# A two-block transformer kernel on one Trainium2 core: the latent attention's input projection taken in two passes over its token tiles, its weights split in the stage in front

## The reference

```python
x = first_block(...)                      # its last step: rms_norm(x_lat, final_g)
for l in range(2):                        # second block
    h = rms_norm_2(x, attn_norm[l])
    proj = h @ w_in[l]                    # gates | latent attention | rwkv | convolution
    c_q, c_kv, k_pe = split(mla_cols, [384, 256, 32])     # 672 columns
    o_a = mla_branch(...)                 # causal attention from c_q, c_kv, k_pe
    ...                                   # o_b: rwkv, o_c: short convolution, gated merge, w_out
    h2 = rms_norm_2(x, mlp_norm[l])
    x = x + square(relu(h2 @ w_up[l])) @ w_down[l]
```

## Time and profile before

| | |
|---|---|
| median of three executions | 4408.32 us |
| the profiled execution: its own time / its span | 4410.29 / 4408.5 us |
| TensorE busy (matmuls / weight loads) | 3905.1 us (89%) / 3036.3 us (69%) |
| VectorE, ScalarE, GpSimd busy | 1842.1 (42%), 1316.5 (30%), 430.7 us (10%) |
| mean granted TensorE clock | 0.926 of full |
| the chain that ended last | PE 74%, DVE 13%, ACT 6%, DMA 3%, POOL 2% |

### The profile page before, as it was taken

One profiled execution on the slowest core, in us unless ns is written; L12 is line 12 of the kernel. 1 busy time (PEld: TensorE's weight loads), 2 busy tenths in 40 slices (PEclk: granted clock), 3 DMA queues, 4 the chain that ended last, 5 costly groups with the idle time before them and its releaser, 6 DMA issues.

```text
span 4408.5 us, 52575 instructions
## 1 busy us (share of the span) xinstructions
PE 3905.1 (89%) x21392; PEld 3036.3 (69%) x21392; DVE 1842.1 (42%) x2826; ACT 1316.5 (30%) x1960; POOL 430.7 (10%) x277
## 2 busy tenths in 40 slices
PE   7788888999997898999788879899988887989999
PEld 3555547888886777788566657678866664767887
DVE  2544433533343334444533254543333335454433
ACT  3332323322233323322324321232232432123222
POOL 0211211000002110000111211000011121100000
PEclk8878889999998999999899989899999998999999
DMA  4112252121121222222111211123311120113332
GB/s 156 55 52 77 77 201 77 48 72 63 58 61 54 78 87 78 86 96 96 54 54 35 74 29 39 49 93 96 96 64 52 36 76 24 44 36 96 93 98 67
DMA packets 320320, 317.03 MB, mean 72 GB/s; under 512 B 8720, under 2 KB 286128, under 8 KB 319952
## 3 DMA queue, kind: packets, MB, share of 16 engines
q1 hardware_dynamic: 320080, 313.67, 22.5%
HBM read 311.55 MB, written 2.10 MB: 71 GB/s over the span
## 4 chain that ended last, share of the span: by engine, by line
PE 74%; DVE 13%; ACT 6%; DMA 3%; POOL 2%; issue 2%; SPq 0%; DVEq 0%; ACTq 0%; POOLq 0%
PE PS L132 73%; DVE scr L146 5%; ACT scr L142 4%; DMA ring<-in_ada_w 1%; DVE PS L160 1%; DVE NBt L156 1%; DVE scr L156 1%; DMA scr<-in_na_bias 1%; PE PS L135 1%; POOL na_w L146 1%; DVE scr L168 1%; DVE scr L164 1%; ACT L142 0%; DVE scr L152 0%; DVE scr L176 0%
## 5 line engine op out<-in xcount | busy, mean ns | idle before, releaser
L132 PE MATMUL PS<-scr 128*32 128x32 f32 (+7 forms) x6692 | 660.2, 284 | 133.7 <-DVE scr L146 77.8
L132 PEld LDWEIGHTS PS<-scr 128*128 128x128 f32 (+4 forms) x6692 | 538.1, 170 | 280.3 <-issue 126.0
L132 PE MATMUL PS<-ffn_h,ffn_w 128*128 128x512 f32 (+1 forms) x3168 | 615.5, 357 | 8.5 <-DVE ffn_h L156 5.7
L132 PEld LDWEIGHTS PS<-ffn_h,ffn_w 128*128 128x128 f32 x3168 | 524.2, 189 | 101.0 <-issue 9.7
L142 ACT ACTIVATE scr<-PS 128x256 f32<-128x256 f32 (+4 forms) x489 | 231.4, 473 | 1015.9 <-PE PS L132 946.7
L146 DVE TENSOR_TENSOR scr<-scr 128x512 f32<-128x512 f32 (+3 forms) x419 | 284.3, 678 | 282.5 <-ACT scr L142 246.6
L132 PE MATMUL PS<-h_h,ring_r 128*128 128x512 f32 (+1 forms) x976 | 365.4, 435 | 40.6 <-POOL ring_r L146 26.0
L132 PE MATMUL PS<-mlp_h,mlp_w 128*128 128x512 f32 x1536 | 364.3, 399 | 5.5 <-DVE mlp_h L146 5.0
L132 PE MATMUL PS<-mlp_g,mlp_w 128*128 128x512 f32 x1536 | 359.7, 396 | 0.0
L132 PEld LDWEIGHTS PS<-mlp_h,mlp_w 128*128 128x128 f32 x1536 | 291.3, 190 | 79.9 <-issue 9.4
L132 PEld LDWEIGHTS PS<-mlp_g,mlp_w 128*128 128x128 f32 x1536 | 288.5, 188 | 69.9
(11 more groups left out here) (150 smaller groups left out, 4739.4 us busy)
## 6 DMA issues: line engine op xcount, KB each, us to landing
ring<-in_ada_w SPq DMA_DIRECT2D x48, 1024.0 KB, 6.8
ring<-in_ffn_w_in SPq DMA_DIRECT2D x44, 1024.0 KB, 5.0
ring<-in_w_up SPq DMA_DIRECT2D x32, 1024.0 KB, 5.5
ring<-in_w_down SPq DMA_DIRECT2D x32, 1024.0 KB, 5.1
ring<-in_w_in SPq DMA_DIRECT2D x60, 512.0 KB, 3.9
ring<-in_ffn_w_out SPq DMA_DIRECT2D x16, 1024.0 KB, 5.0
scr<-in_na_bias SPq DMA_DIRECT2D x32, 512.0 KB, 5.6
ring<-in_na_w_qkv SPq DMA_DIRECT2D x24, 512.0 KB, 4.1
```

The costliest lines, as they stand in the source:

```text
L132: return self.eng.matmul(o, lhsT=l, rhs=r, start=start, stop=stop) if self.eng else Nothing()
```

## The change

`mla_pe` takes the token tiles in two passes: j = 0 and j = 1 for tiles 0, 1, 2, then j = 0 and j = 1 for tile 3 (whose banks it takes and waits for only there), then j = 2 for all four, in the order 3, 0, 1, 2. `mi_k` j now fires when tile 3 has used j. DVE and ACT take the tiles out in the same order 3, 0, 1, 2. `final_pe` puts its sums in banks 4 and 5 and its rows in 6 and 7. The copies (ACT) and subtractions (POOL) of j = 0 and 1 move to the stage in front: on ACT behind the weight split of the last group but one and behind the squares of the last group but one (`f1`), or at the start of the last two groups (`tail`); on POOL in front of the adds of feature tiles 4 and 6. Those of j = 2 stay at the head of `mla`, without the wait for the former stage's PE. `mla_w` moves to memory that is dead from the last `value` (`f1`) or `up` (`tail`) product on, and ACT waits for that product.

```diff
-    M_hi = one_pass("mla_w", 8 * TA + 8200, 8 * 672)
+    M_hi = [one_pass("mla_w", 8 * TA, 2 * 2016)] + [one_pass(f"mla_w{l}", 8 * TA + o, 1344) for l, o in enumerate((4032, 13312))]
@@ ffn_act
             split.act(act, j + 2)
+            if i and j == len(split.specs) - 2:
+                m_in_act(act, 0, 0)
...
                 squares(j, what, f0, n, "na" if i == 0 else "fin")
+                if i and j == len(split.specs) - 2:
+                    m_in_act(act, 0, 1)
@@ ffn_pool
             for n in range(1, 8):
+                if st2 == "fin" and n in (4, 6):
+                    m_in_pool(pool, 0, n // 2 - 2)
@@ final_pe
-        rg = banks(range(8))
+        rg = banks(range(4, 8))
@@ mla_sp: the last slot is freed by
-("mla_in_full", "mi_full", l, 3)
+("mla_in_full", "mi_full", l, M_ORDER[-1])          # M_ORDER = (3, 0, 1, 2)
@@ mla_pe
-        for t in range(4):
-            for g in range(2):
-                o, before = rg.take("mla_in", "mi", l, t, g)
-                emptied(pe, before)
-                outs.append(o)
-        for j, (k0, nk) in enumerate(M_CUT):
-            wl, wh = m_in_parts(l, j)
+        for j, tiles in ((0, (0, 1, 2)), (1, (0, 1, 2)), (0, (3,)), (1, (3,)), (2, M_ORDER)):
+            if j == 0:
+                for t in tiles:
+                    for g in range(2):
+                        o, before = rg.take("mla_in", "mi", l, t, g)
+                        emptied(pe, before)
+                        outs.append(o)
+            (k0, nk), (wl, wh) = M_CUT[j], m_in_parts(l, j)
...
-                for t in range(4):
+                for t in tiles:
...
-            if j < 2:
+            if tiles == (3,):
                 i.then_inc(*pe.up("mla_in_full", "mi_k", l, j))
@@ new
+    def m_in_act(act, l, j):
+
+        act.wait_ge(*loaded("m_in", l, j))
+        act.wait_ge(*(at(*last_up(0)) if l else at("pr_full", "f1", j_value(1), 1, 0)))
+        act.f(m_hi_at(l, j), raw(("m_in", l, j), 672 * M_CUT[j][1]), ACT.Copy).then_inc(*act.up("t_hi", "m_in", l, j))
+
+    def m_in_pool(pool, l, j):
+        wl, wh = m_in_parts(l, j)
+        nk = M_CUT[j][1]
+        pool.wait_ge(*at("t_hi", "m_in", l, j))
+        pool.tt(wl, raw(("m_in", l, j), 672 * nk).rearrange("p (k c) -> p k c", k=nk), wh.bitcast(F32), ALU.subtract).then_inc(*pool.up("t_lo", "m_in", l, j))
@@ mla_act
-        act.after(prev_end(l), "pe")
-        for j, (k0, nk) in enumerate(M_CUT):
-            act.wait_ge(*loaded("m_in", l, j))
-            act.f(M_hi[:, 672 * k0:672 * (k0 + nk)], raw(("m_in", l, j), 672 * nk), ACT.Copy).then_inc(*act.up("t_hi", "m_in", l, j))
+        m_in_act(act, l, 2)
@@ mla_act and mla_dve, front: the tiles are taken out
-            for t in range(4):
+            for t in M_ORDER:
@@ mla_pool: the loop over M_CUT becomes
+        m_in_pool(pool, l, 2)
@@ tail_act
             split.act(act, j + 2)
+            if l == 0 and j >= len(split.specs) - 2:
+                m_in_act(act, 1, j - len(split.specs) + 2)
@@ tail_pool
             for n in range(1, 8):
+                if st2 == "a1" and n in (4, 6):
+                    m_in_pool(pool, 1, n // 2 - 2)
```

More of the change, by code:

```diff
@@ L1484, in j_down, with j_value @@
         return [j for j, g in enumerate(ffn_groups(i)) if g[0] == "down" and g[1] < f0][-1]
+    def j_value(i):
+        return [j for j, g in enumerate(ffn_groups(i)) if g[0] == "value"][-1]
     def ffn_dve(dve, i):
@@ L1940, in program @@
     sc_ = 96 ** -0.5
+    M_ORDER = (3, 0, 1, 2)
     M_CUT = ((0, 3), (3, 3), (6, 2))
@@ L1978, in mla_sp @@
         for j, (k0, nk) in enumerate(M_CUT):
-            stream(sp, ("m_in", l, j), ("mla_in_full", "mi_k", l, j) if j < 2 else ("mla_in_full", "mi_full", l, 3), [(W, k0, nk, 3072, 672)])
+            stream(sp, ("m_in", l, j), ("mla_in_full", "mi_k", l, j) if j < 2 else ("mla_in_full", "mi_full", l, M_ORDER[-1]), [(W, k0, nk, 3072, 672)])
         cv = lambda j: stream(sp, ("cv", l, j), ("cv_full", l, j), [(W, 0, 8, 4768 + 128 * j, 128)])
@@ L2185, in mla_pe, with m_hi_at @@
         pe.end(f"m{l}")
+    def m_hi_at(l, j):
+        return M_hi[0][:, 2016 * j:2016 * j + 2016] if j < 2 else M_hi[1 + l][:, :]
     def m_in_parts(l, j):
@@ L2189, in m_in_parts @@
         o = ev.slot.get(("m_in", l, j), 0) * SLOT
-        return [z.rearrange("p (k c) -> p k c", k=nk) for z in (ringr[:, o:o + 672 * nk], M_hi[:, 672 * k0:672 * (k0 + nk)])]
+        return [z.rearrange("p (k c) -> p k c", k=nk) for z in (ringr[:, o:o + 672 * nk], m_hi_at(l, j))]
+    def m_in_act(act, l, j):
[7 more added lines that the diff above has]
+        pool.tt(wl, raw(("m_in", l, j), 672 * nk).rearrange("p (k c) -> p k c", k=nk), wh.bitcast(F32), ALU.subtract).then_inc(*pool.up("t_lo", "m_in", l, j))
     def mla_act(act, l):
-        act.after(prev_end(l), "pe")
-        for j, (k0, nk) in enumerate(M_CUT):
-            act.wait_ge(*loaded("m_in", l, j))
-            act.f(M_hi[:, 672 * k0:672 * (k0 + nk)], raw(("m_in", l, j), 672 * nk), ACT.Copy).then_inc(*act.up("t_hi", "m_in", l, j))
+        m_in_act(act, l, 2)
         if l == 0:
@@ L2320, in front @@
                 dve.cp(M1k[:, t, :], psum("mla_in", "mi", l, t, 1)[:, 0:288]).then_inc(*dve.up("mla_in", "mi", l, t, 1))
-            dve.wait_ge(*at("mla_made", "m_sq", l, 3))
+            dve.wait_ge(*at("mla_made", "m_sq", l, M_ORDER[-1]))
             dve.ts(ss8, ss8, 1e-6, None, ALU.add, None).then_inc(*dve.up("mla_in", "mn"))
@@ L2985, in last_down, with last_up @@
         return ("pr_full", f"q{l}", 7 + 8 * q, 1, 0)
+    def last_up(l):
+        return ("pr_full", f"q{l}", q_groups().index(("up", 3, 3)), 1, 0)
     def tail_sp(sp, l):
```

## The result

| | before | after |
|---|---|---|
| median of four executions (lowest to highest) | 4407.67 (4404.95 to 4411.08) | 4378.15 us (4371.52 to 4385.14) |
| profiled execution: own time / span | 4410.29 / 4408.5 | 4379.5 / 4377.7 us |
| mean granted TensorE clock | 0.926 | 0.929 |

The ratio is 0.9936, with a 95% interval of 0.992 to 0.9952: 28 us less, between 21 and 35 (the two medians lie 29.5 apart). The forecast was 4383.5, range 4375 to 4391. A second set of six executions, expected at 26 to 30 us less, gave 0.9933 (0.9914 to 0.9951), 29.5 less.

A forecast was written before the change was run, and what follows sets the result against it. PE was taken to wait before both projections for PSUM banks, not data. Layer 0 −15.5, layer 1 −12.3 and clock +3.0 gave −24.8: profiled 4410.29 to 4385.5, median 4383.5 us, range 4375 to 4391.

The forecast's parts named there:

- (1): End of `f1`, layer 0: POOL's moved subtractions block DVE adds, so POOL's last add ends later; cost +4.0 us.
- (2): Layer 0, last add to spread rows: POOL subtracts only j = 2, DVE's two diagonals take 1.4 instead of 8.03; −6.45 us.
- (3): Layer 0: the projection starts on the first low part instead of the last norm instruction; −13.4 us.
- (4): Layer 0's projection: PE never catches up with the norm, and the slow-clock surcharge of 3.0 stays; 0 us.
- (5): Layer 0: `cv 0`, loaded 9 groups later, stands close in front of the position loads; +0.4 us, bounds 0 and 3.9.
- layer 1: last add to the diagonal's end: Layer 1: sqrt goes earlier, POOL's j = 2 still blocks DVE's matrix, which ends at 3294.8 instead of 3295.93; −1.1 us.
- clock behind the hole in front of `cv 1`: Both layers: holes grow to between 2.1 and 4.9 us and the clock drops in one layer of two; +3.0 us.
- A: Position loads 3.9 us, both holes slow, small DVE instruction blocked: gain 17.3, time 4391 us; chance 0.14.
- B: Layer 0's tail, DVE's copies, hangs on something that doesn't move: gain 11.8, time 4396.5 us; chance 0.04.
- C: The norm still holds a bank of tiles 0 to 2, only earlier rows are gained: 4404.7 us; chance 0.04.
- D: Projection clock does not rise while PE takes norm steps as they come: 25 us slower, 4433 us; chance 0.03.
- E: Less blocked in `f1`, or clock up at `cv 1` and at one start: gain 32.7, 4375.6 us; chance 0.09.

The follow-up runs named there:

- low parts on DVE: Changed kernel, but in layer 0 DVE instead of POOL makes the subtractions of j = 0 and 1, behind its adds of feature tiles 5 and 7; 4372.84 us, one execution.
- Passes alone: Kernel before plus only the two passes, new banks and order 3, 0, 1, 2; copies and subtractions stay at the head of `mla`; 4389.13 us, ratio 0.9957.
- splits alone: Kernel before plus only the moved copies and subtractions; one pass over four tiles, former banks and order 0, 1, 2, 3; 4402.4 us, ratio 0.9996.
- old banks: Changed kernel with the final norm's sums and rows put back into banks 0 to 3; 4393.04 us, ratio 0.9972 against before.
- natural order: Changed kernel with the projection's last part and the copies in tile order 0, 1, 2, 3; 4381.24 us, ratio 0.9941 against before.
- all three: Changed kernel with layer 0's low parts on DVE, layer 1's j = 2 subtraction late and tile order 0, 1, 2, 3; 4370.15 us, ratio 0.9918 against before.
- late third subtraction: Changed kernel, but in layer 1 POOL subtracts j = 2 only once the norm's first low part is there; 4387.37 us, one execution.

## Why the prediction was right

It was right in sign and size, and in the mechanism of every step but one: the clock's term came out by luck. Forecast −24.8, measured −28.2 (−21 to −35) on the whole and −27.0 in the two stretches. Step by step:

| step | forecast | measured |
|---|---|---|
| (1) end of `f1`: last split to POOL's last add | +4.0 | 21.72 − 17.53 = +4.19 |
| (2) last add to spread rows | −6.45 | 9.10 − 15.92 = −6.82 |
| (3) spread rows to PE's start | −13.4 | 4.13 − 17.47 = −13.34 |
| (4) 24 groups, slow start kept | 0 | 24.50 − 25.12 = −0.62 |
| (5) position loads | +0.4 | 2.85 − 2.97 = −0.12 |
| layer 1: last add to the diagonal's end | −1.1 | 3.70 − 5.13 = −1.43 |
| layer 1: rows to PE's start | −11.2 | 2.51 − 13.61 = −11.10 |
| clock behind the hole in front of `cv 1` | +3.0 | +2.7 in layer 0, 0 in layer 1 |

(1) The chain came out as walked: copy, subtraction, blocked add, the queue behind it. In layer 1 the moved work cost nothing, as forecast: POOL's last add ends 24.27 us behind the last split, 24.26 before. Both adds ended 0.55 behind POOL (2160.78 + 4.55 = 2165.33, then 2165.88; 2174.70, then 2175.25). By the rule of the Trainium skill (SBUF — State Buffer, Who interferes with whom), that a DVE instruction with two SBUF inputs waits for the whole of GpSimd's, the full 0.69 would be left over; the trace goes by 0.55 in each of these. With the low parts on DVE the last add ended 4.16 earlier again, 3.39 of which reached PE's start.

(2) POOL was done with j = 2 before the small instruction, by 2182.85 − 2182.09 = 0.76 us, 0.5 forecast. That this cover is thin was shown by the low parts on DVE, where it was gone and cost the 1 us named for it. Passes alone show the 8.03 us of the diagonals intact, splits alone 1.42. The subtraction j = 2 took 3.02, and not the 3.3 that were put down for it; in layer 1 that is the whole miss, −1.43 against −1.1.

(3) The largest term and the best one, since it is a difference of two times that both stood in the trace before. It rested on the reading of the banks, which the old banks confirm at 17.47 against 4.13.

(4) PE never waited for a norm step. What was mis-sized is the surcharge of a slow start, kept at 3.0: the clock was up 4.94 us after PE's start, not 6.38, in layer 1 3.49, not 4.96. The 24 groups became 0.6 shorter, and in layer 1 start to copies likewise 0.6 shorter (−13.15 at the copies against −12.53 at the start). I don't claim the change as its cause: the other profiles that start layer 1's projection on a low part have it between 3.49 and 5.17, and natural order, with after's code up to there, has 6.44 in layer 0.

(5) `cv 0` so near to the position loads cost nothing, the lower bound.

The clock: the two holes came out as 4.37 and 3.74, inside the forecast's 2.1 to 4.9, and one layer of two paid, as guessed. But the reading behind the guess was wrong: it took the clock as kept behind layer 1's hole of 2.13, since the next matmul took 0.47, and it fell under the matmuls right behind. So layer 1 had nothing more to lose, whatever its hole, and layer 0 had all. Had both paid, the term would have been double; that it came out is luck. At the copies layer 0 stood at −16.7, at the end of L0 at −14.0: 2.7 against the 3.0. Of the misses (2) and layer 1's diagonal make 0.7, (4) in both layers and (5) 1.8, the clock 0.3. Against them stand 0.2 in (1) and 0.1 each in (3) and in layer 1's start. That makes 2.4, the distance from −24.8 to the −27.2 without the last wait; the wait itself was 0.2 longer in after, which leaves −27.0. The rest of the whole time, 1.2 us, is far inside the interval.

The rivals: A asked for dear position loads; 2.85 us. B asked that DVE's copies hang on something that stays; they moved by 16.7. C is what old banks makes of layer 0, and the change avoids it. (Its reason was worded too widely: the norm's sums are read from banks 4 and 5, in layer 1 from bank 0, but long before the last norm step.) D fell with the windows: 1.00 from the sixth microsecond on. E had its part: of its three causes the slow start came in at 0.6 a layer instead of 3.0 once, and less blocking in `f1` didn't come.

## What to carry to other kernels

When an engine stands in front of a product, look at whether its first operand or its output banks end the wait: here the operand was ready 13 us before, the pass over the tiles with free banks gained 13 us, and in layer 0 placing the norm's rows elsewhere was what made it work. A subtraction moved from POOL's idle time at one place to another takes its block of DVE along, so ask for each new place which DVE instruction will stand and what is queued behind it; if DVE has a pause itself, the same work is cheaper there (3.04 and 3.35 us against 4.43 to 4.55). And a chain that gets shorter in front leaves a larger hole at its next fixed point: size it, since layer 0's, grown from 0.8 to 4.4 us, cost nearly 3 more through the clock. And read the clock from several instructions behind a hole: the first one can still be fast while the clock is about to fall.

## What the hardware showed beyond that

The clock after a hole. In front of `cv 1` the holes fall into three groups over the ten profiles. Behind 0.67 to 1.09 us (layer 0 of before, splits only, natural order, all three) the clock stayed up, four of four. Behind 2.10 to 3.74 (layer 1, every profile) the first matmul took 0.47 or 0.48, and then the clock fell: the first matmul that was slower than its form's usual 0.39 (0.63 for two) started 0.31 to 1.23 us behind the restart, ten of ten. Behind 4.02 to 4.72 (layer 0 of the other six) the first matmul already took 0.76 or 0.77, six of six, as behind 3.20 elsewhere. Against the profiles with small holes the loss in layer 0 cost between 1.4 us (low parts on DVE, old banks) and 2.7 (after). The layers differ in more than the hole: in layer 0 `cv 0` had itself started slow, behind a hole of its own (0.79 behind 5.82), and in layer 1 of after it followed the projection without one. What else counts wasn't tried.

The rise at the start of a projection came between 3.4 and 6.6 us behind the start over all kernels, and an earlier start can meet a later rise. In layer 1 the five profiles that start 32.6 us behind the last split have 3.49 or 3.50; the two with the late third subtraction start at 31.46 and have 4.96, which gave back 0.54 of the 1.15 us gained.

The block works both ways, which the forecast left out: POOL's subtraction of 3.02 took 4.85 where DVE's was running first; it ended 2.88 behind DVE's end (2178.71 against 2175.83), so it stood until 0.14 before that. The Trainium skill (SBUF — State Buffer, Who interferes with whom) has this: the instruction issued first keeps the shared ports and the other one waits for its whole length. The trace agrees here, at 4.85 against 3.02.

Not all small DVE work is blocked alike: beside POOL's subtraction the reciprocal took 0.18, the two with an input in PSUM 0.16 each, while the TENSOR_SCALAR from SBUF, 0.17 when clear, took 1.09 and ended at 2178.73, 0.02 behind POOL's. A POOL subtraction of 128x2016 took 4.43 to 4.55, the same on DVE 3.04 and 3.35. Neither of these is what it takes alone, since each began beside a running add of POOL's and ended 2.12 and 2.11 behind that add's end (2167.71 against 2165.59, 2175.83 against 2173.72). With the 0.14 of overlap that the blocked adds show (0.69 − 0.55) that leaves some 2.26 alone, an estimate that fits DVE's unblocked weight subtractions in the same profile: 1.76 for 128x1536, 2.29 for 128x2048. The adds of 1.3 us on POOL therefore cost DVE 0.8 and 1.1 us.
